# A two-layer encoder trunk on one core: the feed-forward's up projection with the weights as the stationary operand

## The reference: what is computed

```
def rmsnorm(x, g):
    y = x * lax.rsqrt(jnp.mean(jnp.square(x), axis=-1, keepdims=True) + RMS_EPS)
    return y * g
...
    h = x
    for layer in range(DEPTH):                      # DEPTH = 2
        xn = rmsnorm(h, tok_norm_g[layer])
        ...                                         # mix, mo: DeltaNet or gMLP, and attention
        h = h + jnp.concatenate([mix, mo], axis=-1) @ tok_w_out[layer]
        hn = rmsnorm(h, ffn_norm_g[layer])          # (256, 2048)
        h = h + jnp.square(jax.nn.relu(hn @ ffn_w1[layer])) @ ffn_w2[layer]
    return rmsnorm(h, final_norm_g)                 # ffn_w1 (2048, 8192), ffn_w2 (8192, 2048)
```

## Time and profile before

| | |
|---|---|
| median of 3 runs | 2453.8 us (2453.08 to 2455.87) |
| the profiled execution | 2461.26 us |
| its span in the trace | 2459.5 us |
| mean granted clock of TensorE | 0.987 of full |
| PE busy | 2389.2 us, 97% of the span |
| weight loads (PEld) busy | 1997.0 us, 81% |
| DVE busy | 1483.1 us, 60% |
| ACT busy | 1217.7 us, 50% |
| POOL busy | 152.4 us, 6% |
| mean DMA share | 56% (55.8% and 0.2% by queue) |

### The profile page before, as it was taken

The page is one execution under the profiler, slowest core; times in us unless marked ns, Lnnn a source line. Parts: engine busy times, 40 slices in busy tenths (PEclk is TensorE's granted clock), DMA queues, the critical chain, the costliest instruction groups (busy, mean ns, idle before and its releaser), DMA issues. The chain is left out here.

```text
span 2459.5 us, 36207 instructions
## 1 busy us (share of the span) xinstructions
PE 2389.2 (97%) x11371; PEld 1997.0 (81%) x11371; DVE 1483.1 (60%) x2358; ACT 1217.7 (50%) x2117; POOL 152.4 (6%) x119
## 2 busy tenths in 40 slices
PE   7999998898899999999999999999999999999998
PEld 6888787787788888888888888888888888888886
DVE  5646766858767565555665555555666555665554
ACT  4535654555535454444444445554544444444443
POOL 0001112202100000000000000000000000000000
PEclk9989999999999999999999999999999999999999
DMA  6646433333225665666665567565666566666664
GB/s 231 183 111 176 133 103 104 102 106 102 69 85 177 188 184 188 193 193 191 184 184 191 194 185 216 142 183 192 198 184 188 187 193 194 188 188 183 191 193 165
DMA packets 227804, 414.66 MB, mean 169 GB/s; under 512 B 27212, under 2 KB 29149, under 8 KB 227549
## 3 DMA queue, kind: packets, MB, share of 16 engines
q1 hardware_dynamic: 227677, 412.94, 55.8%
HBM read 410.75 MB, written 2.10 MB: 168 GB/s over the span
## 5 line engine op out<-in xcount | busy, mean ns | idle before, releaser
L1274 DVE TENSOR_TENSOR w_lo<-raw,w_hi 128x512 fp32r<-128x512 f32 x1536 | 1083.9, 730 | 657.5 <-ACT w_hi L851 655.6
L851 ACT ACTIVATE w_hi<-raw 128x512 fp32r<-128x512 f32 x1536 | 930.3, 631 | 745.7 <-DMA raw<-in_ffn_w 588.0
L434 PE MATMUL pair<-w_hi,xT_hi 128*128 128x512 f32 x2048 | 819.7, 400 | 17.0 <-DVE w_lo L1274 9.1
L436 PE MATMUL pair<-w_hi,xT_lo 128*128 128x512 f32 x2048 | 803.0, 392 | 0.0
L435 PE MATMUL pair<-w_lo,xT_hi 128*128 128x512 f32 x2048 | 802.0, 392 | 0.0
L434 PEld LDWEIGHTS pair<-w_hi,xT_hi 128*128 128x128 f32 x2048 | 387.9, 189 | 98.9 <-DVE w_lo L1274 10.5
L436 PEld LDWEIGHTS pair<-w_hi,xT_lo 128*128 128x128 f32 x2048 | 387.1, 189 | 83.1
L435 PEld LDWEIGHTS pair<-w_lo,xT_hi 128*128 128x128 f32 x2048 | 388.1, 190 | 77.0 <-issue 0.7
L434 PE MATMUL pair<-w_hi,hid_hi 128*128 128x512 f32 x1024 | 399.3, 390 | 0.0
L436 PE MATMUL pair<-w_hi,hid_lo 128*128 128x512 f32 x1024 | 398.5, 389 | 0.0
L435 PE MATMUL pair<-w_lo,hid_hi 128*128 128x512 f32 x1024 | 398.4, 389 | 0.0
(11 more groups left out here) (201 smaller groups left out, 1209.4 us busy)
## 6 DMA issues: line engine op xcount, KB each, us to landing
raw<-in_ffn_w SPq DMA_DIRECT2D x1024, 256.0 KB, 3.1
raw<-in_dn_w_in SPq DMA_DIRECT2D x208, 256.0 KB, 2.8
raw<-in_tok_w_out SPq DMA_DIRECT2D x128, 256.0 KB, 3.1
raw<-in_gm_w_in SPq DMA_DIRECT2D x112, 256.0 KB, 2.9
raw<-in_mem_w_kv SPq DMA_DIRECT2D x64, 256.0 KB, 3.0
r<-in_mem SPq DMA_DIRECT2D x2, 1024.0 KB, 7.3
h<-in_x SPq DMA_DIRECT2D x2, 1024.0 KB, 6.5
out<-xn_late SPq DMA_DIRECT2D x4, 512.0 KB, 3.9
```

What stands on the lines that cost most here:

```text
L434: pe.matmul(acc, act_hi[:, kt, tokens], w_hi[:, slot], start=start, stop=False)
L436: mm = pe.matmul(acc, act_lo[:, kt, tokens], w_hi[:, slot], start=False, stop=last and k == 1)
L851: act.activation(w_hi[:, slot], raw[:, slot], ACT.Copy).then_inc(hi_ready, 1)
L1274: dve.tensor_tensor(w_lo[:, slot], raw[:, slot], w_hi[:, slot].bitcast(F32), ALU.subtract).then_inc(tiles_split, 1)
```

## The change

The up projection (and it alone) gets matmuls of its own, `up_slab`, for `slab`. The stationary operand is now a 128x128 piece of the weight tile, the moving operand is all 256 tokens of `xT_hi` or `xT_lo`. A weight tile takes 4 pieces `f` by 3 products, 12 matmuls of 256 columns, where it took 6 of 512. The result has hidden features on the partitions: two pieces share one PSUM bank. With it:

- `hidden_transposes` and its waits go. `relu_T` is a view of `relu` with features on the partitions.
- `rstd` is now needed along the free axis. Once a layer ACT makes two diagonal matrices from `rstd` (`rstd_diag`), PE multiplies them by a matrix of ones ahead of slab 7 of the first up block (`rstd_rows`), and ACT copies the result to `rstd_row`, 128x256.
- `relu_result` is DVE's alone: two SCALAR_TENSOR_TENSOR of 512 elements (max with 0, times `rstd_row`), where ACT and DVE had one instruction each.
- ACT makes `hid_hi` from `relu_T` in SBUF, one instruction of 1024 elements for two of 512 out of PSUM; DVE makes `hid_lo` likewise.
- `down` waits, in its first block of a half alone, for `hidden_split`, ahead of each second slab. It waited for `aux_drained` ahead of each slab.

```diff
+            def up_slab(B, s, R, parity):
+
+                for k in range(2):
+                    kt = 2 * s + k
+                    slot = kt % SLOTS
+                    pe.wait_ge(tiles_split, B * 16 + (kt + 1))
+                    for f in range(4):
+                        opens = kt == 0 and f % 2 == 0
+                        if opens:
+                            pe.wait_ge(result_drained[f // 2], R + 1)
+                        acc = banks[2 * parity + f // 2][:, (f % 2) * SEQ:(f % 2 + 1) * SEQ]
+                        hi, lo = (w[:, slot, f * P:(f + 1) * P] for w in (w_hi, w_lo))
+                        pe.matmul(acc, hi, xT_hi[:, kt, :], start=opens, stop=False, skip_group_check=True)
+                        pe.matmul(acc, hi, xT_lo[:, kt, :], start=False, stop=False, skip_group_check=True)
+                        mm = pe.matmul(acc, lo, xT_hi[:, kt, :], start=False, stop=kt == KT - 1, skip_group_check=True)
+                    mm.then_inc(tile_used, 1)
+
+            def rstd_rows(layer):
+
+                n = A_RS[layer]
+                may_fill(pe, n)
+                pe.wait_ge(sem("rstd_diagonal"), 2 * layer + 2)
+                for m in range(2):
+                    mm = pe.matmul(aux[n % 4][:, m * P:(m + 1) * P], ones, rstd_diag[:, m], start=True, stop=True)
+                mm.then_inc(aux_filled[n % 4], 1)
...
-            def hidden_transposes(layer, half, it, j):
-
-                pe.wait_ge(sem("squared"), half * 8 + it * 2 + (16 * layer + j + 1))
-                for q in range(2):
-                    pair_transposes(A_FFN[layer] + 2 * j + q, relu[:, j], q, half * 4 + it)
...
             def hidden(layer, half, it, j):
-                for q in range(2):
-                    n = A_FFN[layer] + 2 * j + q
-                    filled(act, n, half * 4 + it)
-                    act.activation(hid_hi[:, bass.ds(it * 8 + (4 * j + 2 * q), 2), :], pair(n), ACT.Copy
-                                   ).then_inc(sem("hidden_hi"), 1)
+                act.wait_ge(sem("squared"), half * 8 + it * 2 + (16 * layer + j + 1))
+                act.activation(hid_hi[:, bass.ds(it * 8 + 4 * j, 4), :], relu_T[:, j], ACT.Copy).then_inc(sem("hidden_hi"), 1)
...
             def relu_result(layer, B, R, j):
 
-                norm_known(dve, (N_FFN0, N_FFN1)[layer])
+                drained(dve, A_RS[layer])
                 result(dve, B)
-                free_result(dve.tensor_scalar(relu[:, j, 1, :], banks[2 * (R % 2) + 1][:], rstd[:, 0, 1:2], 0.0,
-                                              ALU.mult, ALU.max), 1)
+                for q in range(2):
+                    free_result(dve.scalar_tensor_tensor(
+                        out=relu_T[:, j, 2 * q:2 * q + 2, :],
+                        in0=banks[2 * (R % 2) + q][:].rearrange("p (f t) -> p f t", f=2), scalar=0.0,
+                        in1=over(rstd_row[:], 2), op0=ALU.max, op1=ALU.mult), q)
```

More of the change, by code:

```diff
@@ L242, in encoder_trunk @@
         moT = [memKT[:, layer] for layer in range(2)]
+        relu_T = relu[:].rearrange("p j m (f t) -> p j (m f) t", f=2)
         late_heads = xn_late[:].rearrange("p m (h t) -> p m h t", h=8)
@@ L438, in slab, with first_up @@
                     mm.then_inc(tile_used, 1)
-            def proj_block(B, R, parity, fill=None, between=None):
-                for s in range(SLABS):
[L443 to L447, removed]
+            def up_slab(B, s, R, parity):
[20 more added lines that the diff above has]
+                mm.then_inc(aux_filled[n % 4], 1)
+            def first_up(layer):
+                for s in range(SLABS):
+                    drained(pe, ffn_fill[layer][s])
+                    if s == SLABS - 1:
+                        rstd_rows(layer)
+                    up_slab(B_FFN[layer], s, R_FFN[layer], R_FFN[layer] % 2)
+                    yield
             def transposes(n, pieces, rounds=0):
@@ L1140, in _, with first_up @@
                 operand_hi(mix_fill[0][p], p, GN_OUT)
-            def first_hidden(layer):
-                return lambda: copy_result(B_FFN[layer], R_FFN[layer] % 2, 0, relu[:, 0, 0, :], ACT.Relu,
-                                           (N_FFN0, N_FFN1)[layer])
+            def first_up(layer):
+                for t in range(SLABS):
+                    split(B_FFN[layer] + (t + 2) // 8, (t + 2) % 8)
+                    if t == SLABS - 3:
+                        norm_known(act, (N_FFN0, N_FFN1)[layer])
+                        for m in range(2):
+                            act.activation(rstd_diag[:, m], ident, ACT.Copy, scale=rstd[:, 0, m:m + 1]
+                                           ).then_inc(sem("rstd_diagonal"), 1)
+                    if t == SLABS - 1:
+                        copy_aux(A_RS[layer], rstd_row[:], src=aux[A_RS[layer] % 4][:, 0:SEQ])
+                    yield
             beside(refill(ffn_fill[0], GN_FFN, REFILL_OUT, R_FFN[0]),
-                   chain(out_part(8 * B_OUT[0] + 24, 8), block_steps(B_FFN[0], first_hidden(0))))
+                   chain(out_part(8 * B_OUT[0] + 24, 8), first_up(0)))
             def hidden(layer, half, it, j):
-                for q in range(2):
-                    n = A_FFN[layer] + 2 * j + q
-                    filled(act, n, half * 4 + it)
-                    act.activation(hid_hi[:, bass.ds(it * 8 + (4 * j + 2 * q), 2), :], pair(n), ACT.Copy
-                                   ).then_inc(sem("hidden_hi"), 1)
+                act.wait_ge(sem("squared"), half * 8 + it * 2 + (16 * layer + j + 1))
+                act.activation(hid_hi[:, bass.ds(it * 8 + 4 * j, 4), :], relu_T[:, j], ACT.Copy).then_inc(sem("hidden_hi"), 1)
             def ffn(layer, stages=None, next_steps=None):
@@ L1161, in up @@
                         head(half * 16 + it * 2 + (B_FFN[layer] + j + 1))
-                        copy_result(half * 16 + it * 2 + (B_FFN[layer] + j), (R_FFN[layer] + j) % 2, 0,
-                                    relu[:, j, 0, :], ACT.Relu, (N_FFN0, N_FFN1)[layer])
                     if half == 1:
```

56 lines of the change are left out of this document (27 added, 29 removed).

## The result

| | before | changed |
|---|---|---|
| median (lowest to highest) | 2454.8 us (2453.1 to 2457.4) | 2468.7 us (2468.0 to 2469.5) |
| runs, on one chip | 4 | 4 |
| ratio to before, 95% interval | | 1.0054 (1.0042 to 1.0066) |
| profiled execution's span | 2459.5 | 2466.1 |

The change makes the kernel 13.8 us slower. I had forecast 20 us faster. The sign is that of the rival with the fixed loss, and its time too (2467).

The account below looks back on a forecast made before the run. PE's instruction stream was taken to bound the kernel. Transposes -28.8, matmuls +7.4 and rstd row +1.0 sum to -20.4 us, taken off the median of 2453.8 for 2433 us; range 2414 to 2468.

Parts of the forecast that it names:

- the rival with the fixed loss: Up projection: float32r loss is fixed for each matmul, so 120.0 ns apart, +13.4 us in all, 2467; chance 0.19.
- What bounds the kernel: Everywhere in the feed-forward: PE's own instruction stream, 97% busy, sets the time; other engines count only if PE waits.
- Removed, the transposes: Up blocks: 256 transposes in 32 groups, about 0.9 us each, leave PE's stream; -28.8 us.
- Changed, the matmuls: Up projection: 3072 matmuls at 226.6 ns become 6144 of 256 columns at 114.5 ns; 7.4 us more.
- the first, the load's chain as a lower bound: Up matmuls: a chain of loads takes about 111.8 ns a load, so no distance lies below that.
- The third, that float32r's loss shrinks with the columns: Up matmuls: float32r's own loss, 10 to 11 ns at 512 columns, taken as half of 10.9 at 256.
- The second: Up matmuls: a load hides under a matmul of equal length, as in plain float32 products of 128 columns, 111 ns apart.
- The rival of 111.8: Up projection: float32r loss vanishes or hides, loads set 111.8 ns; -37.0 us in all, 2417; chance 0.24.
- No overlap, or a lower clock: Up projection: loads and streaming don't overlap, or the clock falls; 213 ns a matmul, about +587 us, 3041; chance 0.03.
- Added, the rstd row: PE, two plain products of 128 columns in each of two layers: 0.5 us a layer, 1.0 more, wait free.
- DVE, ACT and POOL, nothing: Behind up blocks: changed relu, square, split and hidden work on these engines adds no time.
- the cover: Behind an up block: tile 4 split after 4.1 us, PE having 5.5 us of split tiles; 1.4 us or more spare.

## Why the prediction was wrong

- **What bounds the kernel: right.** PE at 97% before and after, no wait of PE in the up blocks, and each run's time followed from its distance.
- **Removed, the transposes: right.** -28.8 in the sum, -28.9 on the chip.
- **Changed, the matmuls: the step that failed.** "So I take 106.7 + 2.4 + half of 10.9 = 114.5 ns". It is 120.0: 5.5 ns by 6144 are 34 of the 36 us by which 2433 missed. Of its three arguments, the first, the load's chain as a lower bound, held: the float32r streams bound by 128x128 loads settle at 111.7, and the new distance lies above that. The third, that float32r's loss shrinks with the columns, holds at this width for the matmul with a smaller stationary operand: 113.3 with 64 or 80 columns, 113.4 in the changed kernel so cut. It doesn't shrink in proportion, though, since 13.3 are lost at 384 columns. The second was wrong: plain float32 products of 128 columns, 111 ns apart, were "just the case of the new matmuls". They have as much streaming and as long a load, but they aren't float32r. A float32r stream of 256 columns that could run at 113.3, with a chain of loads that could run at 111.7, runs at 120.0: the overlap that I took as free at equal lengths costs 6.7 ns. I had let a product of another type stand for the new one.
- **The rival with the fixed loss** had the number (120.0, 2467) and the sign. As a mechanism it fell: a fixed loss would not fall by half, from 13.3 to 6.7, when the stationary operand is cut and the 256 moving columns are kept. Its argument, the same loss in every stream whatever stands around it, rested on streams that all had 128-column loads. Its chance of 0.19 was too low: the rows had no float32r stream of 256 columns, and I had one record of 0.18, with a modelled end, to set against it.
- **The rival of 111.8:** the load alone does not set the distance at 256 columns. It does at 192 and less (111.7).
- **No overlap, or a lower clock: no.** The granted clock stood at 0.99 over the run, the level of 2.4 GHz, as before, and loads lie beside the matmuls.
- **Added, the rstd row: right.** 1.0 in the sum, 0.44 in each layer here, and no wait.
- **DVE, ACT and POOL, nothing: right in the result.** A relu piece took 0.69 instead of 0.75; the square got longer, 2.21 for 1.89, and the longest split 2.38 for 2.17. The end of that long split, 4.2 us behind the first relu's start (822.2 to 826.4), agrees with my 4.1 by luck: I had tile 4 held up, but here its split began 0.23 us ahead of the square and was done by 824.1, and it was tile 5's that took 2.38. So PE had tile 4 after 1.9 us, with 4 x 12 x 120.0 = 5.8 in hand, and tile 5 after 4.2, with 7.2: the cover was larger than I had it. At 113.4, with 5.4 in hand for tile 4, PE did not wait either: a block of the kernel with 64 stationary columns takes its 192 distances and no more.
- **The range** ended at 2468, 0.7 us short of the median. With 120.0 the sum gives 2467 off the earlier median, which was 1 us lower than the one beside which the change was run.

## What to carry to other kernels

Swapping the stationary and the moving operand leaves the streamed columns as they are but can halve the width of each matmul and double the loads. In float32r that costs 13.3 ns for each old matmul here (2 x 120.0 for 226.7), and what the swap saves elsewhere has to be weighed against it. So read the new width's distance from a stream of that very type, width and load, and if the trace has none, time one before arguing about its parts. If products share a stationary operand, lay their moving operands side by side for one wide matmul, and, with 128 stationary columns, keep matmuls of equal width together.

## What was unexpected of the hardware

- float32r streams with 128-column loads: 111.7 ns at 128 and 192 moving columns, 120.0 at 256, 146.7 at 320, 173.3 at 384, 202.7 at 448, 226.7 at 512; bf16 has 109.1 and 215.8 at 256 and 512.
- The distance at 256 moving columns depends on the stationary columns, and not in one direction: 120.0 at 128, 113.3 at 80 and 64, 117.8 at 32. At 512 moving columns fewer stationary ones make it longer (226.7 to 230.0 and 231.7).
- With 128 stationary columns widths in turn cost more than each by itself: 353.3 ns a pair of 512 and 256 columns, 350.8 in groups of four, 349.1 in groups of eight, 346.7 by the streams alone. With 64 stationary columns they don't: 340.0 a pair.
- POOL's square and DVE's split hold each other up in both directions. The square that started 0.23 us into a split lasted 2.21 instead of 1.89, and the split behind it 2.38 instead of 0.68. The Trainium skill ("SBUF — State Buffer", section "SBUF: two separate sides") says that whichever of a DVE operation with two SBUF inputs and a GpSimd operation starts first keeps the shared ports for its whole duration, and the other blocks; this trace agrees in both directions, though the square's 0.32 us more is less than the 0.45 that the split still had to run.
